# Recurrence gates by tanh in place of sigmoid, on four quarters of the array, with the activations at other places of a hand-written order

## The reference

```python
def rg_lru_branch(xb, gb, conv_w, conv_b, gate_a_w, gate_a_b, gate_x_w, gate_x_b, lru_lambda):
    xc = conv1d_causal(xb, conv_w) + conv_b           # 4 taps, each channel by itself
    xh = xc.reshape(B, S, 16, 64)
    r = sigmoid(einsum('bshi,hij->bshj', xh, gate_a_w).reshape(B, S, C) + gate_a_b)
    i = sigmoid(einsum('bshi,hij->bshj', xh, gate_x_w).reshape(B, S, C) + gate_x_b)
    log_a = -8.0 * r * softplus(-lru_lambda)
    a = exp(log_a)
    u = sqrt(-expm1(2.0 * log_a)) * (i * xc)
    h = scan(h = a * h + u)                           # over the 256 tokens
    return gelu(gb, tanh form) * h
```

## Time and profile before

| what | value |
|---|---|
| median of 3 runs | 2097.53 us (2097.49 to 2098.7) |
| the profiled execution | 2098.49 us |
| its span | 2096.8 us |
| mean granted clock of TensorE | 0.999 |
| TensorE busy (matmuls) | 2080.1 us, 99% |
| VectorE busy | 1251.4 us, 60% |
| ScalarE busy | 1024.2 us, 49% |
| GpSimd busy | 50.5 us, 2% |
| the mixer of layer 0, 60 to 280 us: busy | TensorE 219.5, VectorE 164.0, ScalarE 152.9, GpSimd 21.7 of 220 us |

### The profile page before, as it was taken

How to read it: one execution, slowest core, us unless ns; L and a number is a source line. 1 busy time by engine, 2 the same in 40 slices (tenths; PEclk the granted TensorE clock), 3 DMA queues, 4 the chain that set the end, 5 groups by cost and what they waited for, 6 DMA issues and landing times.

```text
span 2096.8 us, 29866 instructions
## 1 busy us (share of the span) xinstructions
PE 2080.1 (99%) x10787; PEld 1766.5 (84%) x10787; DVE 1251.4 (60%) x1595; ACT 1024.2 (49%) x1413; POOL 50.5 (2%) x95
## 2 busy tenths in 40 slices
PE   8999999999999999999999999999999999999998
PEld 7888888888888888888888888888888888888886
DVE  5798656556655655655546666566546556655554
ACT  6589555434434544444444444454434434534454
POOL 3010000000000000000000000000000000000000
PEclk9999999999999999999999999999999999999999
DMA  8545656666566666655665554656666666566664
GB/s 256 174 139 156 204 184 187 197 193 190 189 191 192 187 193 190 191 190 183 188 192 183 168 163 151 207 183 190 191 192 185 195 194 189 187 195 189 192 192 148
DMA packets 297966, 390.96 MB, mean 186 GB/s; under 512 B 12272, under 2 KB 205456, under 8 KB 297744
## 3 DMA queue, kind: packets, MB, share of 16 engines
q1 hardware_dynamic: 296656, 385.72, 59.1%
q0 software_dynamic: 944, 3.70, 0.6%
q10 hardware_dynamic: 272, 0.29, 0.0%
HBM read 387.53 MB, written 2.12 MB: 186 GB/s over the span
## 4 chain that ended last, share of the span: by engine, by line
PE 97%; ACT 1%; DMA 1%; DVE 1%; issue 0%; SPq 0%; DVEq 0%; ACTq 0%
PE psum L397 49%; PE psum L422 15%; PE psum L423 15%; PE psum L424 15%; DMA raw<-in_even_w_in_dram 1%; PE psum L456 1%; PE psum L1059 0%; PE psum L1213 0%; PE psum L1255 0%; PE psum L1241 0%; DVE w_split L376 0%; PE psum L1001 0%; ACT cross L493 0%; ACT w_split L369 0%; PE psum L583 0%
## 5 line engine op out<-in xcount | busy, mean ns | idle before, releaser
L376 DVE TENSOR_TENSOR w_split<-raw,w_split 128x1024 fp32r<-128x1024 f32 x728 | 888.0, 1226 | 757.6 <-ACT w_split L369 756.5
L369 ACT ACTIVATE w_split<-raw 128x1024 fp32r<-128x1024 f32 x728 | 767.2, 1059 | 862.9 <-PE psum L424 493.2
L397 PE MATMUL psum<-hg_op,w_split 128*128 128x512 f32 (+1 forms) x6016 | 1060.0, 337 | 1.5 <-DVE total L442 1.5
L397 PEld LDWEIGHTS psum<-hg_op,w_split 128*128 128x128 f32 x6016 | 915.9, 188 | 138.1 <-DVE w_split L376 2.9
L422 PE MATMUL psum<-w_split,ff_op 128*128 128x512 f32 x1264 | 493.2, 390 | 0.5 <-DVE w_split L376 0.5
L424 PE MATMUL psum<-w_split,ff_op 128*128 128x512 f32 x1264 | 491.9, 389 | 0.0
L423 PE MATMUL psum<-w_split,ff_op 128*128 128x512 f32 x1264 | 491.8, 389 | 0.0
L422 PEld LDWEIGHTS psum<-w_split,ff_op 128*128 128x128 f32 x1264 | 237.3, 188 | 49.5 <-DVE w_split L376 0.9
L424 PEld LDWEIGHTS psum<-w_split,ff_op 128*128 128x128 f32 x1264 | 237.3, 188 | 49.4
L423 PEld LDWEIGHTS psum<-w_split,ff_op 128*128 128x128 f32 x1264 | 237.3, 188 | 48.7
L437 ACT ACTIVATE cross<-psum 128x256 f32<-128x256 f32 x188 | 65.5, 378 | 54.7 <-PE psum L397 54.6
(11 more groups left out here) (153 smaller groups left out, 599.2 us busy)
## 6 DMA issues: line engine op xcount, KB each, us to landing
raw<-in_w_up_dram SPq DMA_DIRECT2D x256, 512.0 KB, 3.8
raw<-in_w_down_dram SPq DMA_DIRECT2D x256, 512.0 KB, 3.9
raw<-in_odd_w_in_dram SPq DMA_DIRECT2D x96, 512.0 KB, 3.7
raw<-in_even_w_in_dram SPq DMA_DIRECT2D x56, 512.0 KB, 4.5
raw<-in_even_w_out_dram SPq DMA_DIRECT2D x32, 512.0 KB, 4.6
raw<-in_odd_w_out_dram SPq DMA_DIRECT2D x32, 512.0 KB, 3.7
early_r<-rel_dram POOLq DMA_DIRECT2D x4, 512.0 KB, 6.3
h<-in_x_dram SPq DMA_DIRECT2D x3, 512.0 KB, 8.8
```

Of the source, the lines that this page charges most:

```text
L369: act.activation(w_hi[:, slot], raw[:, rs], ACT.Copy).then_inc(hi_done, 1)
L376: dve.tensor_tensor(w_lo[:, slot], raw[:, rs], w_hi[:, slot].bitcast(F32), ALU.subtract).then_inc(lo_done, 1)
L397: ins = nc.tensor.matmul(o, l, r, start=(k == 0 and n == 0), stop=(k == KT - 1 and n == 1), skip_group_check=True)
```

## The change

- **Sigmoid by tanh.** sigmoid(x) = (1 + tanh(x / 2)) / 2. The gate activations become tanh with half the bias and scale 0.5 (`half_bx`, `half_ba`, made by three small VectorE instructions at key 9). What follows takes the 1/2 and the 1 in: tanh and exp of the gate get a bias beside their scale (`tanh_c`, `decay_c`), GpSimd computes gate x input and adds the input (two instructions a pair, the second waits for the first by `lru_mul`), and VectorE's second product has the factor 0.5. Gate activations, tanh and exp now use one set of tables.
- **Four quarters.** A gate product is 64 rows by 64 columns of the array. Before, the eight products of a pair used the two quarters on the diagonal in turn. Now the order is t, n, e: for the input gate (n = 1) the output goes to the other half of the partitions, so that four products that follow one another stand on four different quarters. The two halves of a tile of n = 0 go to bank 4, those of n = 1 to bank 5. ScalarE turns the halves back: the input gate is activated by two instructions of 64 partitions in place of one of 128.
- **Places.** Gate activations stand at the key of their products, tanh and exp at the same key or one later. Pair 0's recurrence step on VectorE moves from key 36 to 34, pair 1's from 39 to 42, pair 2's from 47 to 46; the third attention group from 33 to 34 with all that hangs on it; pair 2's gate products from 44 to 43; pair 2's convolution from keys 37 and 38 to 39; the gelus of pairs 0 and 1 from 45 and 51 to 52, those of 2 and 3 from 58 to 57. `sigmoid_table_act` goes. GpSimd takes the pairs (0), (1, 2), (3) behind the attention groups 1, 2, 3 in place of (0, 1), (2, 3) behind 1 and 2.

```diff
--- before.py
+++ after.py
@@ -52,17 +52,17 @@
 
 
 
-SWA_FIRST = (13, 23, 33, 45)
+SWA_FIRST = (13, 23, 34, 45)
 SWA_BIAS, SWA_MAX, SWA_EXP, SWA_NORM, SWA_TR, SWA_TRCOPY, SWA_AV, SWA_OUT = 1, 1, (3, 4, 6), 6, 8, 8, 9, 9
 
 
-LRU_CONV = ((29, 29), (33, 33), (37, 38), (42, 42))
-LRU_GATES = (32, 36, 44, 50)
-LRU_SIGMOID = (33, 38, 44, 51)
-LRU_TANH = (34, 39, 46, 53)
-LRU_SQRT = (35, 39, 46, 54)
-LRU_SCAN = (36, 39, 47, 54)
-LRU_OUT = (45, 51, 58, 58)
+LRU_CONV = ((29, 29), (33, 33), (39, 39), (42, 42))
+LRU_GATES = (32, 36, 43, 50)
+LRU_SIGMOID = (32, 36, 43, 50)
+LRU_TANH = (32, 37, 44, 50)
+LRU_SQRT = (33, 41, 45, 52)
+LRU_SCAN = (34, 42, 46, 54)
+LRU_OUT = (52, 52, 57, 57)
 LRU_OUT_LO = 2
 LRU_LAMBDA = 12
 
@@ -159,6 +159,7 @@
         ones = sb("ones", [P, P])
         pcol = sb("pcol", [P, 2, 80])
         lam = sb("lam", [P, 4, NL])
+        half_bx, half_ba = sb("half_bx", [P, NL]), sb("half_ba", [P, NL])
         sinks = sb("sinks", [P, HA])
         mix = sb("mix", [P, MIX])
         early_r = sb("early_r", [P, 2048], F32R)
@@ -272,7 +273,7 @@
 
         lru_xc, lru_gate, lru_act, lru_tanh, lru_a, lru_sqrt, lru_gx = (
             sem("lru_xc"), sem("lru_gate"), sem("lru_act"), sem("lru_tanh"), sem("lru_a"), sem("lru_sqrt"), sem("lru_gx"))
-        lru_tap = sem("lru_tap")
+        lru_tap, lru_mul = sem("lru_tap"), sem("lru_mul")
         lru_hs, lru_gelu, lru_y, lru_yhi = sem("lru_hs"), sem("lru_gelu"), sem("lru_y"), sem("lru_yhi")
 
 
@@ -827,6 +828,10 @@
 
         def lru_par_dve(dve):
             dve.wait_ge(par_pe, 3)
+            for e in range(2):
+                dve.tensor_scalar(half_bx[64 * e:64 * e + 64], psum[64 * (1 - e):64 * (1 - e) + 64, 5, C_BX:C_BX + NL],
+                                  0.5, None, ALU.mult)
+            dve.tensor_scalar(half_ba[:], psum[:, 5, C_BA:C_BA + NL], 0.5, None, ALU.mult)
             dve.tensor_copy(pcol[:, 1, 0:8 * NL], psum[:, 5, 0:8 * NL]).then_inc(par_done, 1)
 
         def lambda_act(act):
@@ -841,10 +846,10 @@
             dve.wait_ge(lam_act, 1)
             link("dve", dve, dve.tensor_scalar(lam[:, 3], pcol[:, 1, C_LAM:C_LAM + NL], -1.0, 0.0, ALU.mult, ALU.max))
             link("dve", dve, dve.tensor_tensor(lam[:, 3], lam[:, 3], lam[:, 2], ALU.add))
-            dve.tensor_scalar(half_c, lam[:, 3], LRU_C / 2, None, ALU.mult).then_inc(lam_act, 1)
-            dve.tensor_scalar(minus_c, lam[:, 3], -LRU_C, None, ALU.mult).then_inc(lam_act, 1)
-
-        half_c, minus_c = lam[:, 0], lam[:, 1]
+            dve.tensor_scalar(tanh_c, lam[:, 3], LRU_C / 4, None, ALU.mult).then_inc(lam_act, 1)
+            dve.tensor_scalar(decay_c, lam[:, 3], -LRU_C / 2, None, ALU.mult).then_inc(lam_act, 1)
+
+        tanh_c, decay_c = lam[:, 0], lam[:, 1]
 
 
         stages = {w: {} for w in ("pe", "act", "dve")}
@@ -1052,19 +1057,16 @@
             pe.wait_ge(swa_pt, 3 * before([k + SWA_TRCOPY for k in SWA_FIRST], key))
             if m:
                 pe.wait_ge(lru_act, 4 * m)
-            for e in range(2):
+            for t in range(2):
                 for n in range(2):
-                    for t in range(2):
-                        d = slice(64 * (e ^ t), 64 * (e ^ t) + 64)
-                        ins = nc.tensor.matmul(psum[d, 4 + t, n * S:(n + 1) * S], gate_w[d, n, 2 * m + t, d], xc[d, m % 2, t],
+                    for e in range(2):
+                        d, to = slice(64 * e, 64 * e + 64), slice(64 * (e ^ n), 64 * (e ^ n) + 64)
+                        ins = nc.tensor.matmul(psum[to, 4 + n, t * S:(t + 1) * S], gate_w[d, n, 2 * m + t, d], xc[d, m % 2, t],
                                                start=True, stop=True)
             ins.then_inc(lru_gate, 2)
 
 
 
-
-        def sigmoid_table_act(act):
-            act.preload_act_table(ACT.Sigmoid)
 
         def lru_gates_act(act, m):
             act.wait_ge(lru_gate, 2 * (m + 1))
@@ -1075,16 +1077,23 @@
                 act.wait_ge(ssq_done, 1)
             for t in range(2):
                 ct = 2 * m + t
-                for n, (dst, bc) in enumerate(((gi, C_BX), (gr, C_BA))):
-                    act.activation(dst[:, t], psum[:, 4 + t, (1 - n) * S:(2 - n) * S], ACT.Sigmoid,
-                                   bias=pcol[:, 1, bc + ct:bc + ct + 1]).then_inc(lru_act, 1)
+                cols = slice(t * S, (t + 1) * S)
+                for e in range(2):
+                    at, to = slice(64 * e, 64 * e + 64), slice(64 * (1 - e), 64 * (1 - e) + 64)
+                    ins = act.activation(gi[to, t], psum[at, 5, cols], ACT.Tanh,
+                                         bias=half_bx[at, ct:ct + 1], scale=0.5)
+                ins.then_inc(lru_act, 1)
+                act.activation(gr[:, t], psum[:, 4, cols], ACT.Tanh, bias=half_ba[:, ct:ct + 1],
+                               scale=0.5).then_inc(lru_act, 1)
 
         def lru_tanh_act(act, m):
             for t in range(2):
                 ct = 2 * m + t
                 act.wait_ge(lru_act, 4 * m + 2 * t + 2)
-                act.activation(g_s[:, t], gr[:, t], ACT.Tanh, scale=half_c[:, ct:ct + 1]).then_inc(lru_tanh, 1)
-                act.activation(g_a[:, t], gr[:, t], ACT.Exp, scale=minus_c[:, ct:ct + 1]).then_inc(lru_a, 1)
+                act.activation(g_s[:, t], gr[:, t], ACT.Tanh, bias=tanh_c[:, ct:ct + 1],
+                               scale=tanh_c[:, ct:ct + 1]).then_inc(lru_tanh, 1)
+                act.activation(g_a[:, t], gr[:, t], ACT.Exp, bias=decay_c[:, ct:ct + 1],
+                               scale=decay_c[:, ct:ct + 1]).then_inc(lru_a, 1)
 
         def lru_sqrt_act(act, m):
             act.wait_ge(lru_tanh, 2 * (m + 1))
@@ -1093,14 +1102,16 @@
         def lru_in_pool(pool, m):
             pool.wait_ge(bias_ready, 8)
             pool.wait_ge(lru_act, 4 * (m + 1))
-            pool.tensor_tensor(gi, gi, xc[:, m % 2], ALU.mult).then_inc(lru_gx, 1)
+            pool.tensor_tensor(gi, gi, xc[:, m % 2], ALU.mult).then_inc(lru_mul, 1)
+            pool.wait_ge(lru_mul, m + 1)
+            pool.tensor_tensor(gi, gi, xc[:, m % 2], ALU.add).then_inc(lru_gx, 1)
 
         def lru_scan_dve(dve, m):
             dve.wait_ge(lru_a, 2 * (m + 1))
             dve.wait_ge(lru_sqrt, m + 1)
             link("dve", dve, dve.scalar_tensor_tensor(g_s, g_a, 1.0, g_s, ALU.add, ALU.mult))
             dve.wait_ge(lru_gx, m + 1)
-            link("dve", dve, dve.tensor_tensor(g_s, g_s, gi, ALU.mult))
+            link("dve", dve, dve.scalar_tensor_tensor(g_s, g_s, 0.5, gi, ALU.mult, ALU.mult))
             for t in range(2):
                 dve.tensor_tensor_scan(hs[:, 2 * m + t], g_a[:, t], g_s[:, t], 0.0, ALU.mult, ALU.add).then_inc(lru_hs, 1)
 
@@ -1142,7 +1153,6 @@
         at_key("dve", LRU_LAMBDA + 2, lambda_dve)
         at_key("pe", 10, v_pe_stage)
         at_key("act", 11, vdup_act)
-        at_key("act", LRU_SIGMOID[0] - 1, sigmoid_table_act)
         for g, k in enumerate(SWA_FIRST):
             at_key("pe", k, swa_qk_pe, g)
             at_key("dve", k + SWA_BIAS, swa_bias_dve, g)
@@ -1495,9 +1505,8 @@
                 swa_norm_pool(pool, g)
                 if g < 2:
                     bias_pool(pool, g + 2)
-                if g in (1, 2):
-                    for m in (2 * g - 2, 2 * g - 1):
-                        lru_in_pool(pool, m)
+                for m in ((), (0,), (1, 2), (3,))[g]:
+                    lru_in_pool(pool, m)
             stick_const_pool(pool)
             for n in range(NF):
                 stick_pool(pool, n)
```

## The result

The changed kernel takes 2114.47 us (median of 6 runs, 2113.59 to 2115.44), the kernel before 2097.70 in the same session (6 runs): 1.0080 times as long, with a 95% interval of 1.0069 to 1.0090. That is 16.8 us slower where 7.8 were forecast, and outside the range. The profiled execution took 2114.22 us with a span of 2112.5.

What follows compares the result with a forecast made beforehand. Bound: TensorE's own instructions, busy 99%. Waits 11.1 less gains 4.2 give 6.9 us, plus 0.9 for the clock: 7.8 on 2098.49 makes 2106.3, less 0.96 to the median: 2105.3 us; range 2101.0 to 2110.0.

Steps and rivals of the forecast that it cites:

- Gate blocks: TensorE's gate products: four run at once, saving 0.86 us of 1.87 a block, 3.45 us over four blocks.
- rival 1: Four gate products never run at once, the 3.45 us gain goes: 2107.9 us, or 2114 if one by one; chance 0.15.
- First wait: TensorE before pair 1's gate block (key 36) waits 4.9 us for VectorE's bias additions of the third attention group.
- Second and fourth wait: TensorE waits for probabilities scaled by GpSimd: 3.1 us before group 3's transposes, 0.8 us behind pair 3's gates and tanh.
- GpSimd two products 2.48: Term in the second wait's chain: GpSimd's two products scaling the probabilities take 2.48 us, ending at 159.1.
- Third: After the attention product, TensorE waits 1.7 us for a low half from VectorE.
- fifth: A gelu load and two gelus before the copies of transposed probabilities on ScalarE make a wait of 0.6 us.
- The clock: TensorE's clock drops behind the first two waits, 0 to 2 us each, partly given back: 0.9 us added.
- Rival 2: The clock is lost at two waits at full price, 2 x 2 us in place of 0.9: 2107.5 us; chance 0.15.

Runs made afterwards that it cites:

- quarters_alone: The kernel before with only the new gate products on four quarters and the input gate's sigmoid in two halves, old places: 2100.18 us (1.0013).
- tanh_alone: The changed kernel with all places as before, tanh table loaded ahead at key 31, old gate products and four 128-partition gate activations a pair: 2099.66 us (1.0010).
- scale_on_vector: The changed kernel with one of the two products that scale each attention group's probabilities moved from GpSimd to VectorE: 2111.18 us (1.0065).
- recurrence_back: The changed kernel with pair 0's recurrence step on VectorE put back from key 34 to key 36: 2116.36 us (1.0090).

## Why the prediction was wrong

The direction, and the place and the kind of the first four waits, were right; most sizes were not, and the price of the clock was far off.

- **Gate blocks: right.** 1.03 us, 0.84 saved each where 0.86 stood; rival 1 is out. That its last sentence comes to 2114, near the measured time, is chance: nothing ran one by one. By the Trainium skill's rule on row tiles and a PSUM bank (TensorEngine Tiling (Array Packing), Restrictions and Gotchas) at most two would have overlapped; here products of both row halves wrote bank 4, on different partitions, and ran four at once. The measurement decides.
- **First wait: 6.0 where 4.9 stood.** TensorE came when forecast (131.4; 132.99 less the 1.65 us of the start is 131.34). VectorE's row from the low half to the last addition took 11.42 us (125.77 to 137.19) where 11.34 stood. What was mis-sized is ScalarE's part:

```profile
119.89 0.95 ACT L1083 ACTIVATE mix<-psum,half_bx 64x256 f32<-64x256 f32 x2
120.87 0.47 ACT L1086 ACTIVATE mix<-psum,half_ba 128x256 f32<-128x256 f32 x1
...
122.72 0.59 ACT L1093 ACTIVATE relu_sq<-mix,lam 128x256 f32<-128x256 f32 x1
123.21 0.59 ACT L1095 ACTIVATE mix<-mix,lam 128x256 f32<-128x256 f32 x1
```

  The gate activations follow one another at 0.49 us where those of 128 partitions did at 0.37, and tanh and exp, with a bias beside their scale, at 0.49 where they did at 0.40: 0.6 and 0.4 us. In quarters_alone sigmoids in halves stand at 0.49 too, and in tanh_alone tanh gates of 128 partitions at 0.36, so the first goes with the split into halves, not with the function. Each lasts 0.47 us in either form; in the split form the next one no longer starts before it ends, also behind one of 128 partitions (120.87 to 121.37). Whether that is for the 64 partitions or for the change of partitions between neighbours, no run separates. My bound of 0.60 for it held; the value taken, 0.37, was too low. I gave the added bias no cost at all; the Trainium skill has one (ScalarE: Activation LUTs, What ACT_TABLE_LOAD costs): about 93 ns for each pointer operand, and the trace agrees with 0.09.
- **Second and fourth wait: 3.3 and 2.6 where 3.1 and 0.8 stood.** The first figure is right by accident: the row behind it ended 3.9 us later than forecast (161.30; 159.1 less 1.65 is 157.45), of which 1.2 are the first wait's, 0.7 the gate block at half rate, 1.0 the turns that GpSimd and VectorE took, and the rest ScalarE's activations again; and TensorE came 3.7 us later, by the clock above all. At the fourth no clock loss stood close ahead, so the lateness showed. In both, "GpSimd two products 2.48" is a term that was mis-sized: it measured 3.46.
- **Third: 2.4 where 1.7 stood; fifth: none** where 0.6 stood. TensorE at half rate gave the copies time, as it seems: in scale_on_vector, at full rate there, 1.3 us came.
- **The clock: 7.4 where 0.9 stood**, the step that failed. Two things were wrong in it. The price: I read 1 to 2 us from the transposes of the start, took part of it as given back and added 0.9 for two waits together; a half-rate stretch costs 1.6 to 3.0 us in these runs, and here it came three times. (Rows 10 were a weak basis: a window over them, 9.80 to 11.42 us, gives a granted clock of 1.00, so they don't show the loss of it.) And the condition: 3.2 us of idling in the earlier trace rows was how long that stretch kept its rate, not the least that loses it. Over the traces of all runs, from 15 us on, none of TensorE's waits of 1.9 us or less brought a half-rate stretch, and all nine of 3.5 us or more did. Of the eighteen between, from 2.35 to 3.38 us, twelve did and six didn't, and not in order of length. The first two of these lines are of recurrence_back, where 3.38 us cost nothing and 2.37 us did (4.55 us for 16 records); the last is of scale_on_vector, where 2.39 us didn't (3.07):

```profile
135.54 1.09 PE L1064 MATMUL psum<-mix 64*64 64x256 f32 x16 [3.38 <-issue]
...
194.05 4.55 PE L398 MATMUL psum<-hg_op,w_split 128*128 128x512 f32 x16 [2.37 <-DVE w_split L377]
...
190.07 3.07 PE L398 MATMUL psum<-hg_op,w_split 128*128 128x512 f32 x16 [2.39 <-DVE w_split L377]
```

  Rival 2 had the right mechanism, with two waits in place of three and a cap of 2 us.
- Waits 3.1 us over and the clock 6.5 over are 9.6 on top of 7.8; the medians show 16.8. The 0.6 between are not accounted for.

What stays open: what decides, for a wait between 2.35 and 3.4 us, whether the clock falls. Nor was it tried what a gate block on four quarters takes if every product has a bank of its own.

## What to carry to other kernels

When a chain of waits is forecast on a kernel whose TensorE is 99% busy, price an idle stretch of 3.5 us or more at its own length and 2 to 3 us more, one of 2.4 to 3.4 us at the same with about two chances in three, and expect the next wait to hide part of that. A work order in which three engines pass buffers round is a whole: undo or move one step and the wait turns up two blocks later, so lay out all engines' rows before a step is moved. And count against each GpSimd instruction that reads SBUF the VectorE instructions with two SBUF operands beside it: both lose.
